# Splitting the down-projection weights of a mixer and MoE step: 20, 3 and 41 pieces instead of 24 and 40, and a step more between load and rounding

## The reference

```python
proj = x @ w_in                                    # 1024 -> u (512), v (512), xs (512)
u = gelu(proj[..., :512]);  v = layer_norm(gelu(proj[..., 512:1024]))
y_a = u * (tril(w_s) applied to v in chunks of 128 tokens, + b_s)
y_b = s5_mixer(xs)                                 # diagonal complex state space, gelu, GLU
x = layer_norm(ALPHA * x + concat(y_a, y_b) @ w_out)
for e in range(16):                                # top 2 of 16 experts for each token
    h = silu(x @ w_gate[e]) * (x @ w_up[e])
    out = out + comb[:, e:e+1] * (h @ w_down[e])   # w_down: 16 x 256 x 1024
x = layer_norm(ALPHA * x + out)
```

## Time and profile before

| | us |
|---|---|
| median of three runs | 1343.06 |
| the profiled execution's own time | 1348.76 |
| its span, first to last instruction | 1347.2 |
| PE busy | 1193.1 (89%) |
| PE weight loads busy | 1014.6 (75%) |
| DVE busy | 919.0 (68%) |
| ACT busy | 525.4 (39%) |
| POOL busy | 473.8 (35%) |

### The profile page before, as it was taken

The page is one execution under the profiler, slowest core; times in us unless marked ns, Lnnn a source line. Parts: engine busy times, 40 slices in busy tenths (PEclk is TensorE's granted clock), DMA queues, the critical chain, the costliest instruction groups (busy, mean ns, idle before and its releaser), DMA issues. The chain is left out here.

```text
span 1347.2 us, 23759 instructions
## 1 busy us (share of the span) xinstructions
PE 1193.1 (89%) x7005; PEld 1014.6 (75%) x7006; DVE 919.0 (68%) x2026; ACT 525.4 (39%) x837; POOL 473.8 (35%) x549
## 2 busy tenths in 40 slices
PE   7999889899978977999999668999999999999920
PEld 6997889778867743888877667888888888888820
DVE  3463875548877746547767777777877787778766
ACT  4131111100002244222322223666666666666564
POOL 3108870100010003322222123455545555545457
PEclk9999999999989988999989778999999999999965
DMA  8689684664335432457888674899999879754495
GB/s 238 185 310 293 183 273 129 190 207 185 126 100 149 132 130 54 158 172 245 272 281 265 230 289 180 254 288 303 288 267 322 263 228 299 226 128 97 103 354 214
DMA packets 142833, 290.04 MB, mean 215 GB/s; under 512 B 54632, under 2 KB 71608, under 8 KB 131472
## 3 DMA queue, kind: packets, MB, share of 16 engines
q1 hardware_dynamic: 126320, 231.99, 50.2%
q0 software_dynamic: 15408, 55.12, 17.6%
q10 hardware_dynamic: 1040, 2.10, 0.5%
HBM read 177.90 MB, written 111.13 MB: 215 GB/s over the span
## 5 line engine op out<-in xcount | busy, mean ns | idle before, releaser
L2193 DVE TENSOR_TENSOR wgu<-w_raw,wgu (+1 forms) x192 | 229.7, 1219 | 84.5 <-ACT wgu L2304 84.2
L2452 PE MATMUL p_gu<-wgu,xg_high 128*128 x768 | 246.2, 402 | 8.0 <-DVE xg_low L2186 4.5
L2304 ACT CAST wgu<-w_raw x188 | 192.7, 1052 | 56.2 <-issue 53.5
L2452 PEld LDWEIGHTS p_gu<-wgu,xg_high 128*128 128x128 f32 x768 | 141.5, 191 | 41.9 <-issue 14.7
L2452 PE MATMUL p_gu<-wgu,xg_low 128*128 x384 | 152.0, 396 | 0.0
L2070 POOL TENSOR_TENSOR spare_e<-nothing 128x1 f32<-128x1 f32 x48 | 46.4, 968 | 216.2 <-DVE yo L2212 216.2
L2071 POOL DMA_INDIRECT acc_rows<-yo,si x48 | 112.3, 2340 | 8.7 <-issue 8.7
L1831 PE MATMUL p_out<-w_out_high,mixt_high 128*128 128x512 f32 x256 | 103.4, 404 | 0.0
L1831 PE MATMUL p_out<-w_out_low,mixt_high 128*128 128x512 f32 x256 | 101.5, 397 | 0.0
L1831 PE MATMUL p_out<-w_out_high,mixt_low 128*128 128x512 f32 x256 | 101.5, 396 | 0.0
L2452 PEld LDWEIGHTS p_gu<-wgu,xg_low 128*128 128x128 f32 x384 | 72.8, 190 | 15.8
(11 more groups left out here) (462 smaller groups left out, 2964.1 us busy)
## 6 DMA issues: line engine op xcount, KB each, us to landing
w_raw<-in_w_gate SPq DMA_DIRECT2D x16, 1024.0 KB, 7.0
w_raw<-in_w_up SPq DMA_DIRECT2D x16, 1024.0 KB, 10.0
wd_high<-w_down_high SPq DMA_DIRECT2D x16, 1024.0 KB, 6.6
wd_low<-w_down_low SPq DMA_DIRECT2D x16, 1024.0 KB, 9.0
ya_u<-in_w_down SPq DMA_DIRECT2D x54, 256.0 KB, 4.2
w_down_low<-ya_r SPq DMA_DIRECT2D x54, 256.0 KB, 6.2
w_down_high<-yb_r SPq DMA_DIRECT2D x40, 256.0 KB, 7.2
acc_rows<-ax SPq DMA_DIRECT2D x18, 512.0 KB, 7.5
```

The lines of the kernel that those rows point to most:

```text
L2193: low = tt(wgu[:, slot, 1, at], raw[:, slot, at], wgu[:, slot, 0, at].bitcast(F32), ALU.subtract)
L2304: nc.scalar.copy(wgu[:, slot, 0, at], raw[:, slot, at]).then_inc(hi_set, 1)
L2452: mm = t.matmul(pg[b][:, :, :], x[:, b, k, :], w[h][:, k], start=(k == 0 and x is xh and h == 0), stop=(k == KD - 1 and x is xl))
```

## The change

In stage A the table UNITS is written out: 20 units instead of 24. From step 16 on there is one unit at most at a step, and rounding, subtraction and stores of the units loaded from step 16 on come one step later (n + 2, n + 3, n + 4). In stage B three units are new, loaded when v tiles 2, 4 and 6 have been produced; ACT rounds them behind the gelu of tiles 5, 7 and 9, DVE subtracts behind the norms of tiles 6, 8 and 10, SP stores at tiles 8, 10 and 12. For that the loop of the gelus on ACT is written out. In stage D there are 41 units: 3, 1, 4, 2, 4, 3, 4, 3, 4, 3, 4, 3, 3 for p = 2 to 14, none at 15. A seventh buffer (`cb_re`, no longer used then) is added. ACT rounds the units of p - 1 between `high(p+2)` and `tile(p)`, where it had rounded those of p behind `score(p-1)`. DVE and SP keep their places.

```diff
-            UNITS, busy = [], {}
-            for n in range(6, 27):
-                free = [s for s in SLOTS if busy.get(s, 0) <= n and n + LIFE <= SLOTS[s]]
-                free.sort(key=lambda s: SLOTS[s])
-                for s in free[:1 + n % 2]:
-                    if len(UNITS) < 24:
-                        UNITS.append((n, s))
-                        busy[s] = n + LIFE
+            UNITS = [(6, "y4"), (7, "y5"), ...
...
-            def units_at(n):
-                return [(j, s, sum(u[1] == s for u in UNITS[:j])) for j, (m, s) in enumerate(UNITS) if m == n]
+            def units_at(n, after=0):
+                return [(j, s, sum(u[1] == s for u in UNITS[:j])) for j, (m, s) in enumerate(UNITS)
+                        if m + (after and after + (m >= LATE)) == n]
...
-                    for j, s, m in units_at(n - 3):
+                    for j, s, m in units_at(n, 3):
...
-                    for j, s, m in units_at(i * FT + f - 1):
+                    for j, s, m in units_at(i * FT + f, 1):
...
-                    for j, s, m in units_at(i * FT + f - 2):
+                    for j, s, m in units_at(i * FT + f, 2):
...
+                for c in range(2, 14):
+                    sp.wait_ge(v_prod, c)
+                    if c % 2 == 0:
+                        half(c // 2 + 1)
+                        if c // 2 - 1 < BUNITS:
+                            unit_in(c // 2 - 1)
+                        if 0 <= c // 2 - 4 < BUNITS:
+                            unit_out(c // 2 - 4)
+                for s in range(BUNITS):
+                    sp.wait_ge(wd_st[s], 32)
...
-                with act.Fori(1, CH // 4 - 1) as i:
-                    for b in range(4):
-                        gelu(i * 4 + b, b, False)
-                for b in range(4):
-                    gelu(CH - 4 + b, b, False)
+                for c in range(4, CH):
+                    gelu(c, c % 4, False)
+                    if c % 2 and c // 2 - 2 < BUNITS:
+                        act.wait_ge(wd_ld[c // 2 - 2], 16)
+                        nc.scalar.copy(wd_hi[c // 2 - 2][:], wd_raw[c // 2 - 2][:]).then_inc(wd_high, 1)
...
+                    if c % 2 == 0 and 1 <= c // 2 <= BUNITS:
+                        j = c // 2 - 1
+                        dve.wait_ge(wd_high, j + 1)
+                        v.tensor_tensor(wd_lo[j][:], wd_raw[j][:], wd_hi[j][:].bitcast(F32), ALU.subtract).then_inc(wd_low, 1)
...
-            STEPS_D, used, left = {}, {}, NUNITS - AUNITS
-            for p in range(2, CH):
-                free = [t for t in range(p) if used.get(t, 0) <= p - 2][:min(3 + (p in (8, 12)), left)]
+            FIRST_D = AUNITS + BUNITS
+            STEPS_D, used, left = {}, {}, NUNITS - FIRST_D
+            for p in range(2, CH - 1):
+                most = 4 if p in (2, 4, 6, 8, 10, 12) else 3
+                free = [t for t in range(-1, p) if used.get(t, 0) <= p - 2][:min(most, left)]
...
                 for p in range(2, CH):
                     if p + 2 <= CH:
                         high(p + 2, p % 2)
+                    units(p - 1)
                     tile(p, p % 2, p // 2)
                     score(p - 1)
-                    units(p)
...
                 turn(CH - 1, 1)
-                units(CH - 1)
                 norm(CH, 0, False, CH // 2)
```

More of the change, by code:

```diff
@@ L150, in hybrid_step @@
         r16 = sb("r16", [P, PAIRS])
+        cb_at = keep.at
         cb_re, cb_im = sb("cb_re", [P, PAIRS, 2, Q]), sb("cb_im", [P, PAIRS, 2, Q])
+        cb_low, cb_high = (sb(f"cb_{n}", [P, PAIRS * 2 * Q], F32R, where=Place(nc, cb_at + i * PAIRS * 2 * Q * 4))
+                           for i, n in enumerate(("low", "high")))
         k_lag_at = keep.at
@@ L217, in hybrid_step @@
             LIFE = 4
-            UNITS, busy = [], {}
-            for n in range(6, 27):
-                free = [s for s in SLOTS if busy.get(s, 0) <= n and n + LIFE <= SLOTS[s]]
-                free.sort(key=lambda s: SLOTS[s])
-                for s in free[:1 + n % 2]:
-                    if len(UNITS) < 24:
-                        UNITS.append((n, s))
-                        busy[s] = n + LIFE
+            UNITS = [(6, "y4"), (7, "y5"), (7, "y6"), (8, "y7"), (9, "x2"), (9, "x3"), (10, "y4"), (11, "y5"), (11, "y6"), (12, "y7"), (13, "x2"), (13, "x3"),
+                     (15, "y5"), (16, "y6"), (17, "y7"), (18, "x2"), (19, "x3"), (22, "y7"), (23, "x2"), (24, "x3")]
+            for s in SLOTS:
+                steps = [n for n, u in UNITS if u == s]
+                assert all(n - m >= LIFE + (m >= LATE) for m, n in zip(steps, steps[1:] + [SLOTS[s]]))
             AUNITS = len(UNITS)
-            assert AUNITS == 24, AUNITS
             wd_ld, wd_st = ({s: phase_sem(f"wd_{k}_{s}") for s in SLOTS} for k in ("in", "stored"))
             wd_high, wd_low = sems("a_wd_high a_wd_low")
-            def units_at(n):
-                return [(j, s, sum(u[1] == s for u in UNITS[:j])) for j, (m, s) in enumerate(UNITS) if m == n]
+            def units_at(n, after=0):
+                return [(j, s, sum(u[1] == s for u in UNITS[:j])) for j, (m, s) in enumerate(UNITS)
+                        if m + (after and after + (m >= LATE)) == n]
             def uses(s):
@@ L855, in hybrid_step @@
             SMP = 10
+            BUNITS = 3
+            u_at = Place(nc, base + 116 * KB)
+            wd_raw = [sb(f"wd_raw{s}", [P, SUP], where=Place(nc, u_at.at + s * 4 * KB)) for s in range(3)]
+            wd_lo = [sb(f"wd_lo{s}", [P, SUP], F32R, where=Place(nc, u_at.at + s * 4 * KB)) for s in range(3)]
+            wd_hi = [sb(f"wd_hi{s}", [P, SUP], F32R, where=Place(nc, u_at.at + s * 4 * KB + 2 * KB)) for s in range(3)]
+            assert pl.at <= u_at.at
+            wd_ld, wd_st = ([phase_sem(f"b_wd_{k}{s}") for s in range(3)] for k in ("in", "stored"))
+            wd_high, wd_low = sems("b_wd_high b_wd_low")
             block = ph.enter_context(nc.Block())
@@ L879, in _, with unit_out, unit_in @@
                     sp.dma_start(toep[:, j, :], k_dram[(L - 1 - j) * Q:(L - 1 - j) * Q + P, :]).then_inc(toep_in, 16)
-                for i in range(2, NH):
-                    sp.wait_ge(v_prod, 2 * i - 2)
-                    half(i)
+                def unit_out(j):
+                    sp.wait_ge(wd_low, j + 1)
+                    u = AUNITS + j
+                    for h, part in enumerate((wd_hi[j % 3], wd_lo[j % 3])):
+                        sp.dma_start(wd_dram[h][u // 4, :, u % 4 * SUP:(u % 4 + 1) * SUP], part[:].bitcast(F32)).then_inc(wd_st[j % 3], 16)
+                def unit_in(j):
+                    u = AUNITS + j
+                    sp.dma_start(wd_raw[j % 3][:], wd_src[u // 4, :, u % 4]).then_inc(wd_ld[j % 3], 16)
+                for c in range(2, 14):
[8 more added lines that the diff above has]
+                    sp.wait_ge(wd_st[s], 32)
                 sp.wait_ge(vs_set, 1)
@@ L1511, in hybrid_step, with raw_of, low_of, high_of @@
             assert left == 0, left
+            def raw_of(t):
+                return ya_u[:, t] if t >= 0 else cb_re[:].rearrange("p a h q -> p (a h q)")
+            def low_of(t):
+                return ya_r[:, t] if t >= 0 else cb_low[:]
+            def high_of(t):
+                return yb_r[:, t] if t >= 0 else cb_high[:]
             def landed(p, of, each):
@@ L1558, in units_in @@
                     for u, t in STEPS_D[p]:
-                        sp.dma_start(ya_u[:, t], wd_src[u // 4, :, u % 4]).then_inc(wd_ld[p % 2], 16)
+                        sp.dma_start(raw_of(t), wd_src[u // 4, :, u % 4]).then_inc(wd_ld[p % 2], 16)
                 def units_out(p):
@@ L1565, in units_out @@
                             sp.dma_start(wd_dram[h][u // 4, :, u % 4 * SUP:(u % 4 + 1) * SUP],
-                                         (yb_r, ya_r)[h][:, t].bitcast(F32)).then_inc(wd_st[p % 2], 16)
+                                         (high_of, low_of)[h](t).bitcast(F32)).then_inc(wd_st[p % 2], 16)
                 for p in range(2, CH + 1):
@@ L1577, in _ @@
                 for b in range(2):
-                    sp.wait_ge(wd_st[b], landed(CH - 2 + b, 2, 32))
+                    sp.wait_ge(wd_st[b], landed(CH + b, 2, 32))
                 for s in (x1_stored, ax1_stored):
@@ L1685, in units @@
                 def units(p):
+                    if p not in STEPS_D:
+                        return
                     act.wait_ge(wd_ld[p % 2], landed(p, 2, 16))
                     for u, t in STEPS_D[p]:
-                        nc.scalar.copy(yb_r[:, t], ya_u[:, t]).then_inc(wd_high, 1)
+                        nc.scalar.copy(high_of(t), raw_of(t)).then_inc(wd_high, 1)
                 for p in range(2, CH):
@@ L1788, in units @@
                 def units(p):
+                    if p not in STEPS_D:
+                        return
                     dve.wait_ge(wd_high, landed(p, 1, 1))
                     for u, t in STEPS_D[p]:
```

(2 more changed lines are left out.)

## The result

The changed kernel takes 1334.37 us, the median of six runs (1330.06 to 1336.47). The kernel before took 1345.26 beside it, median of six (1341.97 to 1349.26). The ratio is 0.9919, 95% interval 0.9905 to 0.9933, so 10.9 us less. The forecast was 1317 us; the time lies 0.4 above the top of the range. "Faster by over 0.5%" came true.

The account below looks back on a forecast made before the run. Time to be had lay in A and D, where PE is full but for waits and the clock they cost. -13.3 (A) + 5.1 (B) - 20.8 (D) = -29.0 gave 1314.1 to 1319.8, middle 1317 us; range 1308 to 1334.

Parts of the forecast that it names:

- A: Stage A, second half: later rounding ends ACT's idle ahead of `high`, so PE's two long waits go; -13.3 us.
- Both long waits: A, steps 19 and 23: PE waits 3.07 and 3.70 us for v_im; with lost clock 6.33 and 6.97 us too long.
- the small waits: A: PE waits under 1 us, put at 1.5 us in all, forecast to stay; bound -14.8 if they go too.
- The rival that DVE itself would keep one long wait: A: DVE's products at 0.94 us beside POOL hold v_im, one long wait stays; +6.6, 1324 us, chance 0.12.
- B: Stage B: three DVE subtractions add 1.8 us, the gate of tile 9 waits 3.3, clock loss costs 3.3; +5.1 us.
- D up to turn(14): Stage D, turn(9) to turn(14): earlier `high` and later roundings let PE hold 13.61 us a tile; -11.9 us.
- It fits: D: DVE's 27.1 us for two tiles fits PE's 27.2, with a few us of slack, so the pace holds.
- DVE's 27.1 us for two tiles: D: two norms, two x1t, seven units, one select and 3 us of root waiting, against PE's 27.2.
- the root's part: D: DVE's waiting for POOL's root, estimated at 3 us in two tiles.
- D's end: D, turn(16): no units at tile 15 ahead of the norm, so T + 21.9 instead of T + 30.8; -8.9 us.
- The DMA rival: D: the queue carries only about 280 GB/s, two tiles take 31 us; 1336 us, chance 0.12.
- the rival of no effect: Waits move to the next load, for instance because SP issues it later still; 1340 us, chance 0.06.

Follow-up runs that it names:

- b_pool: Changed kernel with B's three subtractions of units moved from DVE (VectorE) to POOL (GpSimd), behind its roots of tiles 6, 8 and 10: 1333.07 us.
- d_lru: Changed kernel with D's places reused after three tiles or later and SP waiting for the stores of tile p-3 instead of p-2: 1320.85 us.
- d_lru_wait2: d_lru with only SP's wait put back to the stores of tile p-2, same places and counts: 1332.22 us.
- d_small_loads: Changed kernel with D's 41 unit loads cut to 16 of 128 partitions, so it doesn't compute the layer: 1316.38 us.
- four orders: Changed kernel, and it with D's old order, with units rounded ahead of high, or with even-tile units subtracted behind select: 1334.37, 1333.41, 1336.34, 1333.27 us.

## Why the prediction was right in A and B and wrong in D

*A.* Right in mechanism, -13.7 for -13.3. Both long waits and their clock went. The sum is as close as it is by luck: the two long steps gave 5.1 and 7.0 us where 6.3 and 7.0 were forecast, since a wait of 1.02 stays in the first, and two of the small waits, which were to stay, went and gave 1.3. The rival that DVE itself would keep one long wait is out: DVE keeps up once ACT is not late.

*B.* Right in mechanism and nearly in size: wait 3.36 for 3.3, clock lost, +4.2 for +5.1. The wait is 1.84 of the 4.2; the clock cost the other 2.4 and not 3.3, and in two of nine profiles it cost nothing. b_pool adds that the work does not get cheaper on GpSimd.

*D up to turn(14): the step that failed.* The prediction said of a load: "ACT asks for it the better part of a tile (13.6 us) later, and x1 of p comes only then", and from that: "It fits". It timed the issue of the load by x1 alone. The code has a second wait at the same place, for the stores of two tiles ago, and the profile shows it to end last: 4.2 and 9.7 us behind x1. ACT then asked 0.8 us after the issue of the load of tile 8 instead of a tile later. By d_lru against d_lru_wait2 that wait is worth 13.5 us of D. What counts is when the load lands: in d_small_loads SP still issues up to 6.5 us behind x1, but the small loads land soon, and D is 17.2 us shorter than in the changed kernel.

The trace of the kernel before had shown the second wait already. x1 of tile 15 was set at 751.26 (749.98 + 1.28), and the load came 7.0 us later, 0.07 behind the landing of the last store of tile 13 (758.17):

```profile
758.24 1.28 SPq L1559 DMA_DIRECT2D ya_u<-in_w_down  x3
```

For tiles 9, 10 and 11 it was 2.5, 1.5 and 1.6 us.

*DVE's 27.1 us for two tiles.* In the changed kernel x(8) starts at 638.09 and x(10) at 669.48, 31.4 us apart. The sum lacked the wait at the rounding (3.61) and 2.1 us of a select that runs beside POOL; the root's part was right (2.3 us in these two for 3.0). In d_lru from x(9) at 646.35 to x(11) at 674.09 it is 27.7 with eight units. The sum was right for a case that the kernel wasn't in.

*D's end.* turn(16) waited 2.39 us instead of 7.45, by the step as the prediction had it. But from turn(14) to turn(16) there are 28.3 us, 2.4 less than the 30.8 before, for 8.9 forecast. Even in d_small_loads there are 23.5, so 8.9 was 1.6 too much by itself.

*The DMA rival* gave 1336 us, and the time was 1334. Its number was right by luck and its mechanism wrong: it took 280 GB/s for a ceiling, and 27 us of D ran at 329 with the wait moved.

*Its forecast of the whole.* With the ring opened the same change reaches 1320.85 us (d_lru), and 1316.42 with one unit in B instead of three, where 1317 had been forecast. What was missing was not in the change's order but in its buffers' reuse. No term and no bound priced SP's wait for the stores; only the rival of no effect named the queue ("because SP issues it later still"), at a chance of 0.06 and with the gain of A left out, which made its 1340 too long. The range ended at 1334 since I left the upper half of the DMA case out.

## What to carry to other kernels

When a load's place is reused, its issue has two conditions, the trigger and the landing of what left that place. Compare the issue time in the queue's timeline with both before you give a load "a tile of time". If reordering several engines leaves a stage at one length (here four orders, 229.3 to 230.4 us), look for a ring through a queue, and check in each order whether the ring is what holds it. A low rate can be the effect of such a ring (here 264 GB/s for 378), so compare it with what the same queue reaches elsewhere. Waiting for the stores of one more tile back was worth 13.5 us of D here; the three other orders of ACT and DVE, with the short wait, were worth nothing.

## Seen on the way

A short operation of DVE can take many times as long beside POOL. The same comparison on 8 elements per partition takes 1.25 us in a select beside `low`, and 0.17 in one without:

```profile
657.71 1.29 POOL L1631 TENSOR_TENSOR mixt_low<-ya,mixt_high 128x512 fp32r<-128x512 f32 x1 [9.59 <-ACT mixt_high L1695]
657.77 1.25 DVE L1774 TENSOR_TENSOR s_gq<-s_gq,s_red 128x8 f32<-128x8 f32 x1
...
688.89 0.17 DVE L1774 TENSOR_TENSOR s_gq<-s_gq,s_red 128x8 f32<-128x8 f32 x1
```

Two such operations make select 8.5 us instead of 6.36. The Trainium skill (SBUF — State Buffer, SBUF: two separate sides) says that DVE and GpSimd hold their shared port pair for a whole instruction. The trace agrees: the comparison starts 0.06 us behind POOL's subtraction (657.71) and ends with it (659.02 and 659.00). It cost the kernel nothing measurable: d_lru and d_small_loads have it and keep PE's pace.
